# A hybrid layer with product-key experts on one core: two weight buffers that begin 64 bytes later

## The reference

```python
def _layer(x, p_i, ...):                      # block 1
    proj = _rmsnorm(x, g_mix) @ w_in          # q, k, v, gates of two mixers
    o_a = gated_delta_rule(...)               # 4 heads, chunks of 64
    o_b = mlstm_chunkwise(...)                # 4 heads
    x = x + (sigmoid(gate_a) * (o_a @ w_branch_a) + sigmoid(gate_b) * (o_b @ w_branch_b)) @ w_out
    x = x + (silu(h @ w1) * (h @ w3)) @ w2    # h = _rmsnorm(x, g_ffn)
    return x + sigmoid(_rmsnorm(x, g_ple) @ w_ple_gate) * (p_i @ w_ple)

# block 2: rglru_mixer (a linear recurrence), then peer_ffn
# block 3: fox_mixer (attention with forget gates), then peer_ffn

def peer_ffn(h, q_w, subkey1, subkey2, expert_u, expert_v):   # per token, 8 heads
    # the 16 best of 128 x 128 experts by the sum of two key scores
    act = gelu(einsum('thkd,td->thk', u, xc))
    return einsum('thk,thkd->td', softmax(top_s) * act, take(expert_v, expert))
```

## Time and profile before

| | us |
|---|---|
| median of 3 runs | 2524.07 (2521.89 to 2526.58) |
| the profiled execution | 2525.84 |
| its span | 2524.1 |
| TensorE busy (matmuls) | 2453.1 |
| VectorE busy | 1831.7 |
| ScalarE busy | 1246.8 |
| GpSimd busy | 1230.0 |

### The profile page before, as it was taken

How to read it: one execution, slowest core, us unless ns; L and a number is a source line. 1 busy time by engine, 2 the same in 40 slices (tenths; PEclk the granted TensorE clock), 3 DMA queues, 4 the chain that set the end, 5 groups by cost and what they waited for, 6 DMA issues and landing times.

```text
span 2524.1 us, 47109 instructions
## 1 busy us (share of the span) xinstructions
PE 2453.1 (97%) x18074; PEld 2275.1 (90%) x18074; DVE 1831.7 (73%) x3366; ACT 1246.8 (49%) x2150; POOL 1230.0 (49%) x525
## 2 busy tenths in 40 slices
PE   7999999989899999999999999999999999999999
PEld 7999999988899999998888888889999999888887
DVE  6857783668749899987777775563997999555555
ACT  6345543455555544444444454555454444444444
POOL 5547787645679977760000014456997676100000
PEclk9999999989999999999999998999999999999999
DMA  5435787732456655548777763334665454566664
GB/s 172 137 93 184 239 318 254 266 117 83 135 176 193 201 159 155 156 143 280 253 252 258 257 193 100 101 109 151 198 194 174 155 158 153 184 192 192 192 192 142
DMA packets 126063, 457.94 MB, mean 181 GB/s; under 512 B 13984, under 2 KB 15392, under 8 KB 125600
## 3 DMA queue, kind: packets, MB, share of 16 engines
q1 hardware_dynamic: 118512, 425.56, 53.4%
q10 hardware_dynamic: 7344, 29.49, 3.3%
HBM read 453.95 MB, written 1.05 MB: 180 GB/s over the span
## 4 chain that ended last, share of the span: by engine, by line
PE 84%; DVE 9%; issue 3%; ACT 2%; DMA 1%; POOL 1%; SPq 0%; DVEq 0%; POOLq 0%; ACTq 0%
PE mm L1297 28%; PE ms L1337 28%; PE mm L812 17%; PE ms L1318 3%; DVE work L1994 1%; POOL low L1937 1%; DVE hs L1994 1%; PE ms L819 1%; DVE work L1988 1%; PE ms L827 1%; DVE scratch L1994 1%; DVE work L1991 1%; PE mm L981 1%; PE mm L819 1%; DVE mm L1988 0%
## 5 line engine op out<-in xcount | busy, mean ns | idle before, releaser
L1937 POOL TENSOR_TENSOR low<-ring,high 128x1024 fp32r<-128x1024 f32 (+2 forms) x502 | 1216.2, 2437 | 915.3 <-ACT high L1548 758.7
L1802 ACT ACTIVATE high<-ring 128x1024 fp32r<-128x1024 f32 x506 | 535.8, 1059 | 355.6 <-PE ms L1337 324.6
L1297 PE MATMUL mm<-hs,high 128*128 128x256 f32 x4096 | 520.4, 280 | 3.4 <-ACT high L1548 3.4
L1337 PE MATMUL ms<-high,wts 128*128 128x512 f32 x2048 | 510.8, 392 | 0.0
L2573 DVE TENSOR_TENSOR low<-ring,high 128x1024 fp32r<-128x1024 f32 x256 | 313.4, 1225 | 248.3 <-ACT high L1802 248.3
L1297 PEld LDWEIGHTS mm<-hs,high 128*128 128x128 f32 x4096 | 486.8, 188 | 3.8 <-issue 3.8
L1337 PEld LDWEIGHTS ms<-high,wts 128*128 128x128 f32 x2048 | 384.2, 188 | 84.0
L1548 ACT ACTIVATE high<-ring 128x1024 fp32r<-128x1024 f32 (+2 forms) x252 | 258.2, 1030 | 126.5 <-PE mm L812 98.1
L812 PE MATMUL mm<-hs,high 128*128 128x256 f32 x2192 | 286.3, 284 | 7.5 <-DVE parts L1988 3.9
L812 PEld LDWEIGHTS mm<-hs,high 128*128 128x128 f32 x2192 | 268.2, 191 | 12.9 <-ACT high L1548 7.2
L1337 PE MATMUL ms<-low,wts 128*128 128x512 f32 x1024 | 276.1, 391 | 3.0 <-DVE low L2573 3.0
(11 more groups left out here) (342 smaller groups left out, 3070.0 us busy)
## 6 DMA issues: line engine op xcount, KB each, us to landing
ring<-w_peer_experts SPq DMA_DIRECT2D x512, 512.0 KB, 3.9
work<-w_mod ACTq DMA_DIRECT2D x48, 512.0 KB, 5.6
ring<-w_late_mods SPq DMA_DIRECT2D x48, 512.0 KB, 4.5
ring<-w_ffn_up SPq DMA_DIRECT2D x44, 512.0 KB, 5.1
ring<-w_peer_q SPq DMA_DIRECT2D x32, 512.0 KB, 3.7
ring<-w_fox_in SPq DMA_DIRECT2D x32, 512.0 KB, 3.5
ring<-w_lru_in SPq DMA_DIRECT2D x22, 512.0 KB, 3.5
ring<-w_gates SPq DMA_DIRECT2D x16, 512.0 KB, 3.6
```

The costliest lines, as they stand in the source:

```text
L1297: ins_ = pe.matmul(mm[:, s_ % BANKS, 0:T], w_[:, k * P:(k + 1) * P], hs[:, b_, k, :], start=pass_ == 0 and k == 0, stop=pass_ == 2 and k = ...
L1337: ins_ = pe.matmul(ms[:, 2 * c + half, :], wts[:, s_ % 3, b_, c * P:(c + 1) * P], v_[:, half * 512:(half + 1) * 512], start=s_ == 0 and pa ...
L1802: act.activation(high[:, (q0 + i) % CUT, :], ring[:, n_ % RAW, :], ACT.Copy) \
L1937: pool.tensor_tensor(low[0:rows, cut_slot, 0:width], ring[0:rows, raw_slot, 0:width], high[0:rows, cut_slot, 0:width].bitcast(F32), ALU.su ...
```

## The change

Two small tensors of 16 float32 values per partition, 64 bytes each, are declared, one ahead of `high` and one behind `low`. Nothing reads or writes them. They are there for the space that they take.

```diff
@@ -443,8 +443,10 @@
 
         ring = sb("ring", [P, RAW, SLOT])
 
+        sb("shift", [P, 16])
         high = sb("high", [P, CUT, SLOT], F32R)
         low = sb("low", [P, CUT, SLOT], F32R)
+        sb("shift_back", [P, 16])
         x = sb("x", [P, KD, T])
```

## The result

The changed kernel takes 2569.0 us in the median of four runs (2565.8 to 2570.3) against 2525.3 for the kernel before beside it. The ratio is 1.0166, with a 95% interval from 1.0149 to 1.0183. It is slower by 44 us, outside the range, and by more than the slower rival's first price of 29 us.

A forecast was written before the change was run, and what follows sets the result against it. TensorE's matmuls were taken to bound the kernel. Every term was 0, so the span stayed 2524.1 us and the forecast was 2524 us against the median, with a range from 2506 to 2540 us.

The forecast's parts named there:

- slower rival: L1297, the expert_u loop: equal halves give 118 ns instead of 113.3; 29 us, 2553 us, with L1337 also 2574; chance 0.10.
- What bounds the kernel: Whole kernel: TensorE holds 84% of the chain; matmul lines L1297, L1337 and L812 hold 73% of the span on it.
- The pair of rows with 258 columns: Two norms' matmuls on `raw`, opposite against equal places: 1.93 against 1.92 us for 16, taken as no effect.
- The term for 256 moving columns: L1297 and L812: no change, bounded by 1.3 ns a matmul, 14 us to either side.
- Equal against opposite: Operand pairs modulo 128: `high` against `hs`, `parts`, `wts` goes from opposite to equal; against `ring`, `high` and `low` the reverse.
- The paces: 256-column matmuls: 113.3 ns fast and 118 ns slow, 4.7 ns apart; the first expert loop at the fast one.
- the faster rival: Clash of streams before: equal halves speed L812 by 11 us and L1337 by 7; 2506 us, half of it 2515; chance 0.17.
- signs named for being wrong: L1337's twelve at 2.72 or 2.83 us, L812 at one pace, L1297 at 2.83 us, or TensorE waiting for `low`.
- The lottery: L812: about half of 4632 matmuls slow; all fast would give 11 us, a redealing 2 to 3 us of either sign.
- ScalarE, VectorE, GpSimd: Work on `high` and `low`: no change; steps stay at 1.06, 1.23 and 2.41 us, GpSimd's cover 0.1 us a step.
- The GpSimd rival: First expert loop: GpSimd bounds from a 2.51 us step; 2539 us at +10%; chance 0.10, shared with a dearer redealing.
- The rule of the Trainium skill: TensorE's operand reads: two independent ports, so no address could matter and the TensorE part would be exactly nothing.

The follow-up runs named there:

- fine sweep: Streams alone without the computation, moving operand 0 to 240 bytes after the stationary one in steps of 16; 256 columns: 120.0 ns at 0, 113.3 at 112.
- experiment 1: Streams alone without the computation, stationary and moving tensors at all pairs of places in steps of 32 bytes; 256 columns at equal places: 120.0 ns a matmul.
- experiment 3: Against the kernel before, `hs` moved from 64 to 0 modulo 128, its two pads also moving `wts` by 128 bytes: 2583.6 us, ratio 1.0226.
- experiment 5: Streams alone without the computation, one stationary tensor and moving tensors 0 to 240 bytes further in steps of 16; 512 columns: 226.7 ns at 0.
- experiment 6: Against the kernel before, `high` and `low` 128 bytes later, everything behind them 256 later: 2561.5 us, ratio 1.0166.
- experiment 8: Against the kernel before, `hs` 112 bytes behind `high`, `wts` 112 before it: 2525.5 us, ratio 0.9991; then `wts` at distance 0 instead: 2512.6 us, ratio 0.993.
- experiments 2: Against the kernel before, only the first small tensor: `high`, `low` and everything behind them 64 bytes later: 2522.9 us, ratio 0.9985.
- experiment 4: Against the kernel before, `wts` alone moved from 64 to 0 modulo 128, equal to `high`: 2521.2 us, ratio 0.998.
- the last kernel: Against the kernel before, `hs` 112 bytes behind `high` modulo 256 and `wts` at distance 0 from `high`: 2512.6 us, ratio 0.993.

## Why the prediction was wrong

**What bounds the kernel: right.** TensorE's pace was read from starts, and nearly all of the result is in that pace. One operand of nearly all matmuls does lie in the shifted buffers. To suspect the two streams that TensorE reads at once was right as far as the runs go: the distance between them sets the pace. That their reads clash is not shown.

**The pair of rows with 258 columns: the step that failed.** The term for 256 moving columns was nothing, within 14 us to either side; it measured 35.5 us in the expert_u loop and 15.1 in the projections. It came from the earlier trace rows, which compares `raw` parts at 64 and at 0 modulo 128 and finds no difference; I called it the nearest row, took its value and gave it a bound of 14 us. But seven of its eight matmuls begin 8 to 56 bytes off a multiple of 64. The fine sweep shows what such a row is worth: at 0, 16, 32 and 48 bytes the paces are 120.0, 118.6, 116.7 and 118.3, mean 118.4; at 192 to 240 they are 117.8 or 113.3, 116.7 or 119.2, 118.3 and 117.0, mean 116.3 to 118.1. Off the multiples of 64 the paces are alike on both sides. In the sweep 113.3 needs an exact distance, 192 or 112, and of the `raw` rows with 258 columns at most the first of a part stands at one. The earlier trace rows itself had the sign: 1.93 us for 16 is 120.6 ns, neither 113.3 nor 118, and more than two columns can add. In the changed kernel these matmuls kept their pace, 120.6 ns after 120.4 (means of the starts under 130 ns apart), while those on `raw` with 256 columns went from 116.9 to 119.9. I had written that the likeness was not exact, and still let it set both the value and the bound. The bound was also too narrow for what the rows print: two differences of starts given to 0.01 us can be off by 0.02 together, 2.5 ns a matmul. The loss per matmul in the expert_u loop was 5.8 ns.

**Equal against opposite: half right.** The table of places was modulo 128. The unit is 256 bytes, as experiments 1, 3, 5 and 6 show. For this change both take the pairs from unequal places to equal ones, so this did not cost the forecast, but in experiment 3 it did cost an expectation: "keeps its place modulo 128" is no safe layout.

**The paces: their number was wrong.** I took 113.3 and 118 as the only two and priced the slower rival with 4.7 ns a matmul. Equal places have a third, 120.0, which the earlier trace rows could not show, since both streams there stand at distance 192. In the expert_u loop that is 35.5 us instead of 29.

**The slower rival: right in place and kind, too small, and given 0.10.** It let the expert_v loop only get slower, and the faster rival let both widths get faster. In fact each got one: 256 columns became slower, and the loop with 512 took 5.3 us less, where the forecast had no change. A forecast that has one answer for "clash" could not say this. Two of the signs named for being wrong came true: twelve matmuls of the expert_v loop in 2.72 us, and a single pace in L812.

**The lottery: right that it exists, too large.** Half of L812's matmuls was the estimate. In the kernel before, 984 of its 3288 matmuls that move `hs` have the next one 116 to 120 ns behind them, and 644 of the 1344 that move `parts`. In the changed kernel nothing of it is left, because 120.0 is the only pace at distance 0. The mean of the starts under 130 ns apart went from 114.8 to 119.9 ns on `hs` and from 115.8 to 119.8 on `parts`, worth 16 and 5 us. What is missing to 11.3 and 3.8 came back by shorter pauses between the streams on `hs` and by fewer matmuls at the lower clock on `parts`.

**ScalarE, VectorE, GpSimd: right.** 1059, 1225 and 2408 ns, and TensorE waits no more for `low` than before (0.5 us). The GpSimd rival did not come up. It had been priced too high: the 53 steps of the earlier trace rows average 134.6 / 53 = 2.54 us, and a tile takes 2.72, so the cover was 0.18 us a step and not 0.1.

**The rule of the Trainium skill** ("SBUF — State Buffer", "Who interferes with whom": two independent read ports, so no contention within TensorE) would have made the sum nothing. The measurement decides: with all other engines at rest, a stream of 256 columns takes 113.3 to 120.0 ns a matmul, and in experiments 1 and 5 only the places of its two operands and what ran ahead of it differ.

**What stays open.** Why these distances. The paces at 2.4 GHz are 272, 283 and 288 cycles for 256 columns, 16, 27 and 32 more than the columns, but no run here looks inside. No stream was run that keeps its weights, so that the loading of new ones takes part is a guess. Whether pieces and rows with other steps than 512, and 1024 or 2048 bytes, have the same table wasn't tried, nor what in the work ahead of a stream chooses between its two paces, beyond the streams behind three float32 matmuls. Each kernel was profiled in one execution, so how often a loop falls into either pace isn't known.

## What to carry to other kernels

Where TensorE is the bound and every matmul loads new weights, the bytes at which the two operands begin, relative to each other modulo 256, are a free setting: here the worst choice cost 2.3% (experiment 3) and the best gained 0.7% (experiment 8). List them for the hottest loops, and check the layout again whenever a buffer is added ahead of them. Read the pace from start to start in a saturated stretch and compare it with columns times cycle time; two paces for one form of instruction mean that something other than the instruction sets it. A row is a near likeness only if it agrees in what is being questioned, here the exact alignment, and a small kernel of bare streams tells in one run what no row of the big one can.

## What the runs showed of the hardware

A stream of float32r matmuls, each with its own weights, at a granted clock of 1.00 loses 6 to 13% against one column per cycle (106.7 ns for 256 columns): 113.3, 117.8 or 120.0 ns are the commonest paces. With 512 columns it takes 226.7 to 234.4 ns against 213.3. At the lower level, 1.2 GHz, the one such stretch looked at lost nothing: in the changed kernel, at a granted clock of 0.50, 16 matmuls of 256 columns took 416.17 - 412.62 = 3.55 us, of which the first alone 0.36 us; the others are 213 to 214 ns apart, 256 cycles at that level, with operands at distance 0:

```profile
412.62 3.76 PE L814 MATMUL mm<-parts,high 128*128 128x256 f32 x16
416.17 1.91 PE L814 MATMUL mm<-parts,low 128*128 128x256 f32 x8
```

In the bare streams a pace is reached within about seven matmuls, with 512 columns at equal places within six to ten, and kept to the end of the stream. At distances of 32, 64, 160, 192 and 208 bytes, and with 512 columns at 112, two paces were seen, in the streams or in the kernels' loops. The runs of one kernel lie apart by different amounts: 20 us in the four of experiment 6, 21 us in the 23 of the kernel before that stood beside experiments 2 to 4, 5 us in the six of the last kernel. That the choice of paces makes this spread is not shown.
